# Attention scores two groups ahead of the transposes in a two-block transformer kernel

## The chip, the cores and the metric

The kernel runs on one core of a Trainium2 chip. The metric is the time of one execution on the device in microseconds (us), lower is better. In profile rows PE is TensorE, PEld its weight loads, DVE VectorE, ACT ScalarE, POOL GpSimd and SP SyncE.

## The reference, cut to what matters

Two transformer blocks run one after the other over 512 tokens of width 1024. The change lies in the mixing part of the first block, which is computed for each of its two layers.

```python
def first_block(x, norm_mix, w_in, q_norm, ...):
    for l in range(DEPTH):                       # DEPTH = 2
        h = rmsnorm(x, norm_mix[l])
        proj = jnp.einsum('btd,de->bte', h, w_in[l])
        q, k, v, u, ug, ga, gb = jnp.split(proj, SPLITS, axis=-1)
        ...
        a_out = sliding_window_attention(q, k, v, sinks[l])   # window 128, 16 heads, 2 kv heads
        c_out = conformer_conv(u, ug, conv_w[l], ...)         # 31 taps, layernorm, silu, w_pw
        merged = jax.nn.sigmoid(ga) * a_out + jax.nn.sigmoid(gb) * c_out
        x = x + jnp.einsum('btd,de->bte', merged, w_out[l])
        ...                                      # gated feed-forward
```

In the attention a query block of 128 tokens sees its own and the previous block of keys; the first block of a sequence has no previous one. The softmax has one extra logit for each head, the sink.

## The kernel before, in words

**Layout.** Channels lie on the 128 partitions and tokens on the free axis. Weights stream in as 351 chunks of 128x1024. ScalarE rounds each to `wh` (`round_chunk`), GpSimd subtracts to get the rest `wl` (`rest`), and TensorE multiplies a chunk (`tile`) as 8 x 3 products of 128x512 into one of the eight PSUM banks. Semaphores order the engines; each engine runs its own list of instructions as written, so the code's order is the engine's order.

**Stages of a layer.** Eight chunks for the convolution's input `u`, one for `k`, eight for `q`, one for `v`, sixteen gate chunks, four for the convolution's output (`out(0)` to `out(7)`, two halves of a chunk each, operand `ch` and `cl`), eight for `w_out`, then the feed-forward part.

**The convolution's taps.** Channel tiles 2 and 3 and part of tile 0 are summed on VectorE, one instruction a tap, into banks 6, 7 and 5 (`taps`). The first `SPLIT` taps of tile 0 and all of tile 1 are products on ScalarE (`products`) and additions on GpSimd (`add_tap`). `conv_ready` counts tiles 2, 3 and the joined tile 0.

**Attention groups.** There are 16 groups g of four heads and one block n = g % 4. For each, TensorE computes the scores (`scores`, into banks 0 and 1 or 2 and 3 in turn), VectorE the maxima (`maxima`), ScalarE the exponentials (`exps`), VectorE normalises `prob` (`normalise`), TensorE transposes it into banks 4 and 5, ScalarE copies that out (`turned_out`), TensorE multiplies with `v` in bank 7, and ScalarE copies the result (`pv_out`). A group with n = 0 has one key block, and half the work.

**What is woven in.** Between the transposes of a group and its product with `v` TensorE computes one gate tile in bank 6. VectorE reads it (`gate`, signals `gate_free`), ScalarE takes its tanh and then rounds the next chunk. The layer norm of the convolution (sum, mean, squares, variance, root, product, silu, rounding to `ch`, rest `cl`) is spread over groups 4 to 10, its two sums of TensorE also in bank 6. In the last three groups the output tiles `out(m)` take the gate tiles' place in bank 6: VectorE frees the bank with `gate_conv(m)` (signal `co_out`), and `out(m + 1)` waits for that. Then come `merge`, `merged_hi` and `merged_rest`, which make the operand of `w_out`.

In the lines that follow `LN_EARLY` is 2 and `CO_FROM` 13.

```python
for g in range(16):                       # TensorE, before, without the layer norm
    if g < 15:
        scores(g + 1)
    if g >= CO_FROM:
        out(2 * (g - CO_FROM), 6)
    ...                                   # transposes of group g
    if 1 <= g < CO_FROM:
        tile(c, c % RW, 6, hh, hl)        # gate tile g + 3
    if g >= CO_FROM:
        out(2 * (g - CO_FROM) + 1, 6)
    ...                                   # product of group g with v
```

## Time and profile before

| | us |
|---|---|
| median of three runs | 2336.82 (2336.79 to 2336.86) |
| the profiled execution | 2334.86 |
| its span, first to last instruction | 2332.6 |
| TensorE busy | 2271.0 (97%) |
| VectorE busy | 1137.1 (49%) |
| ScalarE busy | 993.5 (43%) |
| GpSimd busy | 981.8 (42%) |

The span leaves out what lies around the first and last instruction. Matmuls overlap, so a busy TensorE is not one at its peak; what a waiting TensorE loses is read from its idle time. The attention groups of layer 0 lie from 157 to 311 us of the span, those of layer 1 from 869 to 1024 us. A last column in square brackets is the idle time of the engine ahead of a row and what ended it.

### The profile page before, as it was taken

The page shows a single profiled execution, that of the slowest core. Times are in us where ns is not written, and L with a number is a line of the kernel's source. Part 1 is how long each engine was busy: PE and PEld are TensorE (multiplying, and loading weights), DVE is VectorE, ACT ScalarE, POOL GpSimd, SP SyncE. Part 2 cuts the span into 40 slices and gives each one's busy share as a digit, 9 for nine tenths or more (in the row PEclk, how much of TensorE's full clock was granted, in tenths as well). Part 3 has the DMA queues.
Part 4 walks back from the last instruction along what each step waited for, and adds up shares of the span by engine and source line. Part 5 has one row for each costly group of instructions (what it writes and reads, how often), then busy time and mean ns, then how long its engine had stood idle before and what let it go on. Part 6 is the DMA issues. An engine that isn't in the chain of part 4 may idle for free.

```text
span 2332.6 us, 29198 instructions
## 1 busy us (share of the span) xinstructions
PE 2271.0 (97%) x10536; PEld 1791.9 (77%) x10560; DVE 1137.1 (49%) x1475; ACT 993.5 (43%) x1499; POOL 981.8 (42%) x453
## 2 busy tenths in 40 slices
PE   6989999999999999999999999999999999999999
PEld 5866678888888876678888888876777667888887
DVE  5876664222334785666222334647776443433300
ACT  4546643333223545744333213335535663444311
POOL 4962234444443882234444443432442113544442
PEclk9999999999999999999999999999999999999999
DMA  4321123333662221122333472322121002333332
GB/s 151 91 64 56 62 73 91 99 92 97 192 221 73 90 73 54 55 70 88 96 98 98 150 247 90 91 81 64 55 83 53 28 28 72 107 93 97 99 92 88
DMA packets 59842, 216.00 MB, mean 93 GB/s; under 512 B 6640, under 2 KB 6896, under 8 KB 59760
## 3 DMA queue, kind: packets, MB, share of 16 engines
q1 hardware_dynamic: 52272, 187.62, 26.0%
q10 hardware_dynamic: 7488, 27.27, 3.5%
q8 instruction: 54, 0.88, 0.2%
q14 instruction: 28, 0.23, 0.0%
HBM read 212.76 MB, written 2.10 MB: 92 GB/s over the span
## 4 chain that ended last, share of the span: by engine, by line
PE 88%; DVE 7%; ACT 4%; issue 2%; DMA 0%; SPq 0%; DVEq 0%; ACTq 0%
PE bank L1276 26%; PE bank L1278 25%; PE bank L1277 25%; PE bank L1732 1%; PE bank L1410 1%; PE bank L1289 1%; PE bank L1736 1%; PE bank L1470 1%; PE bank L1350 1%; PE bank L1450 1%; PE bank L1720 1%; PE bank L1345 1%; PE bank L1306 1%; ACT prob L479 1%; DVE root L749 1%
## 5 line engine op out<-in xcount | busy, mean ns | idle before, releaser
L307 POOL TENSOR_TENSOR wl<-raw,wh 128x1024 fp32r<-128x1024 f32 x351 | 855.7, 2438 | 1304.3 <-ACT wh L380 1304.1
L1276 PE MATMUL bank<-hh,wh 128*128 128x512 f32 x2024 | 816.3, 403 | 32.9 <-DVE hl L763 19.4
L1277 PE MATMUL bank<-hl,wh 128*128 128x512 f32 x2024 | 792.9, 392 | 0.0
L1278 PE MATMUL bank<-hh,wl 128*128 128x512 f32 x2024 | 792.8, 392 | 0.0
L380 ACT ACTIVATE wh<-raw 128x1024 fp32r<-128x1024 f32 x351 | 369.7, 1053 | 641.8 <-PE bank L1278 610.0
L1276 PEld LDWEIGHTS bank<-hh,wh 128*128 128x128 f32 x2024 | 383.1, 189 | 128.7 <-issue 28.6
L1277 PEld LDWEIGHTS bank<-hl,wh 128*128 128x128 f32 x2024 | 383.2, 189 | 86.3 <-issue 9.8
L1278 PEld LDWEIGHTS bank<-hh,wl 128*128 128x128 f32 x2024 | 382.7, 189 | 81.4
L1276 PE MATMUL bank<-ah,wh 128*128 (+1 forms) x528 | 208.0, 394 | 0.0
L1278 PE MATMUL bank<-ah,wl 128*128 (+1 forms) x528 | 207.0, 392 | 0.0
L1277 PE MATMUL bank<-al,wh 128*128 (+1 forms) x528 | 204.9, 388 | 0.0
L1007 DVE TENSOR_TENSOR tmp<-bank,rstd 128x512 f32<-128x512 f32 x44 | 30.4, 692 | 198.3 <-PE bank L1278 198.3
L327 POOL TENSOR_TENSOR conv<-conv,th 128x512 f32<-128x512 f32 x90 | 118.3, 1315 | 17.4 <-ACT th L428 10.5
L1278 PEld LDWEIGHTS bank<-ah,wl 128*128 128x128 f32 x528 | 99.1, 188 | 23.2
L1277 PEld LDWEIGHTS bank<-al,wh 128*128 128x128 f32 x528 | 99.1, 188 | 22.2
L1276 PEld LDWEIGHTS bank<-ah,wh 128*128 128x128 f32 x528 | 99.3, 188 | 19.7
L796 DVE SCALAR_TENSOR_TENSOR bank<-glu,par,bank 128x512 f32<-128x512 f32 x148 | 111.6, 754 | 4.0
L549 ACT ACTIVATE ah<-tmp 128x512 f32 x44 | 27.8, 632 | 193.8 <-DVE tmp L1010 193.8
L1019 DVE SCALAR_TENSOR_TENSOR ada_acc<-ada_w,cond,ada_acc 128x1024 f32<-128x1024 f32 x42 | 59.3, 1412 | 94.4 <-DMA ada_w<-ada 94.1
L1005 DVE TENSOR_TENSOR tmp<-bank,rstd 128x512 f32<-128x512 f32 x44 | 30.4, 692 | 101.2 <-PE bank L1278 100.7
L479 ACT ACTIVATE prob<-bank,neg_max,q_scale 128x256 f32<-128x256 f32 (+1 forms) x128 | 67.2, 542 | 19.7 <-DVE neg_max L885 19.7
L546 ACT ACTIVATE tmp<-tmp 128x512 f32<-128x512 f32 x44 | 27.8, 632 | 109.5 <-DVE tmp L1005 109.5
(318 smaller groups left out, 2571.9 us busy)
## 6 DMA issues: line engine op xcount, KB each, us to landing
raw<-stream SPq DMA_DIRECT2D x351, 512.0 KB, 3.6
ada_w<-ada ACTq DMA_DIRECT2D x48, 512.0 KB, 4.6
x<-x_t ACTq DMA_DIRECT2D x4, 512.0 KB, 7.8
out_t<-x SPq DMA_DIRECT2D x8, 256.0 KB, 2.1
cst<-consts SPq DMA_DIRECT2D x1, 640.0 KB, 11.1
tmp<-masks SPq DMA_DIRECT2D x1, 320.0 KB, 11.3
par<-params SPq DMA_DIRECT2D x1, 253.0 KB, 4.6
cst<-consts SPq DMA_DIRECT2D x1, 224.0 KB, 8.0
```

Of the source, the lines that this page charges most:

```text
L307: nc.gpsimd.tensor_tensor(wl[:, slot, :], raw[:, raw_slot, :], wh[:, slot, :].bitcast(F32), ALU.subtract).then_inc(lo_ready, 1)
L327: nc.gpsimd.tensor_tensor(conv[:, tile_, :], conv[:, tile_, :], th[:, 0, 4 + (p - 1 - tile_) % 4, :], ALU.add).then_inc(tap_added, 1)
L380: af(wh[:, slot, :], raw[:, raw_slot, :], ACT.Copy).then_inc(hi_ready, 1)
L479: af(prob[:, g % 2, i, lo:], bank[:, b + kv, (i % 2) * 2 * P + lo:(i % 2 + 1) * 2 * P], ACT.Exp, bias=neg_max[:, g % 2, i:i + 1], scale=q_ ...
L546: af(tmp[:, 2 + p, :], tmp[:, 2 + p, :], ACT.Silu).then_inc(ffn_silu, 1)
L796: link(stt(acc, glu[:, t, j:j + T], w, acc, ALU.mult, ALU.add))
L1005: tt(tmp[:, 2 + p, :], bank[:, b, :], rstd[:, :], ALU.mult).then_inc(lin_free, 1)
L1007: tt(tmp[:, 4 + p, :], bank[:, b + 1, :] if b < 3 else bank[:, 0, :], rstd[:, :], ALU.mult).then_inc(lin_free, 1)
L1019: stt(acc, w, c_k, acc, ALU.mult, ALU.add).then_inc(ada_used, 1)
L1276: mm(dst, wh[:, slot, w], xh, start=start, stop=False)
L1277: mm(dst, wh[:, slot, w], xl, start=False, stop=False)
L1278: return mm(dst, wl[:, slot, w], xh, start=False, stop=stop)
```

## The change

Scores, maxima, exponentials and normalising run two groups ahead of the transposes instead of one, and TensorE issues the next scores behind the transposes of a group instead of ahead of them. Two gate tiles instead of three are computed ahead of the first scores; tiles 2 and 3 follow the first two score groups, in banks 6 and 4. The layer norm is spread over groups 3 to 12. Tile 0 of the convolution gives 20 instead of 16 taps to ScalarE and GpSimd. In the last three groups VectorE normalises ahead of `gate_conv`. The code that is left out of the diff repeats these edits.

```diff
@@ -222,8 +222,8 @@
...
-        EARLY_GATES = 3
-        CO_FROM = 16 - EARLY_GATES
+        EARLY_GATES, AHEAD = 2, 2
+        CO_FROM = 13
...
@@ -236,15 +236,16 @@
...
-        TAPS_U, TAPS_Q = [2, 3, 4, 4, 4, 4], [4, 4, 3, 3, 5, 5, 5, 5]
-        SPLIT, LN_EARLY = 16, 2
+        TAPS_U, TAPS_Q = [2, 3, 4, 2, 4, 5], [5, 4, 3, 4, 5, 5, 5, 5]
+        SPLIT = 20
...
-        PRODUCTS_AT = {2: 3, C_K: 2, C_Q: 4, C_V: 2, C_GATE: 2, C_GATE + 1: 2, C_GATE + 2: 1}
+        PRODUCTS_AT = {2: 3, C_K: 2, C_Q: 4, C_V: 4, C_GATE: 2, C_GATE + 1: 3, C_GATE + 2: 2}
...
-        ADDS_AT = {2: 1, C_K: 2, C_V: 2, C_GATE: 2, C_GATE + 1: 2, C_GATE + 2: 2}
+        ADDS_AT = {2: 1, C_K: 2, C_V: 4, C_GATE: 2, C_GATE + 1: 4, C_GATE + 2: 2}
...
+        LN_SUM, LN_MEAN, LN_SQUARES, LN_VAR, LN_ROOT, LN_NORM, LN_HI, LN_REST = 3, 5, 6, 8, 9, 10, 11, 12
...
@@ -490,6 +491,10 @@
...
                 exps(0)
+                exps(1)
+                gate(2)
+                products(C_GATE + 2)
+                gate(3)
                 for g in range(16):
...
-                    if g < 15:
-                        exps(g + 1)
-                    if g == 7 - LN_EARLY:
...
-                    if g == 9 - LN_EARLY:
...
-                    if g == 11 - LN_EARLY:
...
-                    if g == 12 - LN_EARLY:
...
-                    else:
-                        gate(g + EARLY_GATES)
+                    elif g:
+                        gate(g + 3)
...
@@ -868,8 +873,6 @@
...
                 gate(1, M_V % 4)
-                taps(5)
-                gate(2, M_SWAP[7] % 4)
                 taps(len(own) - tapped[0])
                 join_split()
...
                 maxima(0)
+                maxima(1)
+                gate(2, 6)
                 normalise(0)
+                normalise(1)
+                gate(3, 4)
                 for g in range(16):
...
-                    if g < 15:
-                        maxima(g + 1)
-                    if g == 6 - LN_EARLY:
...
-                    if g == 7 - LN_EARLY:
...
+                    if g == LN_SQUARES:
...
-                    if g == 10 - LN_EARLY:
+                    if g == LN_ROOT:
                         invert(tmp[:, 5, :], root[:, :])
-                    if g == 11 - LN_EARLY:
...
+                    if g + AHEAD < 16:
+                        normalise(g + AHEAD)
                     if g < CO_FROM:
-                        normalise(g + 1)
-                        if g == 12 - LN_EARLY:
+                        if g:
+                            gate(g + 3, 6)
+                        if g == LN_REST:
                             for t in range(CT):
                                 out_rest(t)
-                        gate(g + EARLY_GATES, 6)
...
-                        if g < 15:
-                            normalise(g + 1)
                         merge(m + 1)
...
@@ -1387,7 +1394,6 @@
                 last.then_inc(vt_turned, 1)
                 tile(c0 + C_GATE + 1, (c0 + C_GATE + 1) % RW, M_V % 4, hh, hl)
                 pe.wait_ge(lin_free, m0 + M_SWAP[7] + 1)
-                tile(c0 + C_GATE + 2, (c0 + C_GATE + 2) % RW, M_SWAP[7] % 4, hh, hl)
...
                 scores(0)
-                pe.wait_ge(conv_ready, (CT - 1) * l + 2)
-                tile(c0 + C_GATE + EARLY_GATES, (c0 + C_GATE + EARLY_GATES) % RW, 6, hh, hl)
+                scores(1)
+                pe.wait_ge(conv_ready, (CT - 1) * l + 1)
+                tile(c0 + C_GATE + 2, (c0 + C_GATE + 2) % RW, 6, hh, hl)
                 pe.wait_ge(root_ready, ROOTS * l + 3)
+                tile(c0 + C_GATE + 3, (c0 + C_GATE + 3) % RW, 4, hh, hl)
                 for g in range(16):
                     n, j = group(g)
-                    if g == 7 - LN_EARLY:
...
-                        pe.wait_ge(gate_free, 16 * l + g + EARLY_GATES)
...
-                    if g < 15:
-                        scores(g + 1)
                     if g >= CO_FROM:
                         out(2 * (g - CO_FROM), 6)
                     pe.wait_ge(probs_ready, 16 * l + g + 1)
-                    if g:
+                    if g == 0:
+                        pe.wait_ge(conv_ready, (CT - 1) * (l + 1))
+                    else:
                         pe.wait_ge(turned_out, 16 * l + g)
+                    if g == 1:
+                        pe.wait_ge(gate_free, 16 * l + 4)
                     for w in range(1 if n == 0 else 0, 2):
...
                     last.then_inc(turned, 1)
-                    if g == 7 - LN_EARLY:
+                    if g + AHEAD < 16:
+                        scores(g + AHEAD)
+                    if g == LN_MEAN:
                         pe.wait_ge(mean_out, l + 1)
-                    if g == 9 - LN_EARLY:
+                    if g == LN_VAR:
...
                     if 1 <= g < CO_FROM:
-                        pe.wait_ge(gate_free, 16 * l + g + EARLY_GATES)
-                        c = c0 + C_GATE + g + EARLY_GATES
+                        pe.wait_ge(gate_free, 16 * l + g + 3)
+                        c = c0 + C_GATE + g + 3
                         tile(c, c % RW, 6, hh, hl)
...
-                    if g == 0:
-                        pe.wait_ge(conv_ready, (CT - 1) * (l + 1))
```

**TensorE at the start of the groups**, from the first scores to the first product with `v`. `win_mask` rows open a score group, `k,q` rows are scores, `hh,wh` opens a gate tile, `cst,prob` rows are transposes and `prob_t,v` the product. Before:

```order
L1405 MATMUL bank<-win_mask,ident_bf 128x512 [waits lin_free,gate_free,k_ready,consts_ready]
...
L1410 MATMUL bank<-k,q 128x128 x4
L1276 MATMUL bank<-hh,wh 128x512 [waits lo_ready,conv_ready]
...
L1405 MATMUL bank<-win_mask,ident_bf 128x512 [waits gate_free,root_ready]
...
L1450 MATMUL bank<-cst,prob 128x128 [waits probs_ready]
...
L1470 MATMUL bank<-prob_t,v 64x256 [waits turned_out,conv_ready]
```

And now:

```order
L1411 MATMUL bank<-win_mask,ident_bf 128x512 [waits lin_free,k_ready,gate_free,consts_ready]
...
L1411 MATMUL bank<-win_mask,ident_bf 128x512 [waits gate_free]
...
L1416 MATMUL bank<-k,q 128x256 x4
L1283 MATMUL bank<-hh,wh 128x512 [waits lo_ready,conv_ready]
...
L1283 MATMUL bank<-hh,wh 128x512 [waits lo_ready,root_ready]
...
L1460 MATMUL bank<-cst,prob 128x128 [waits conv_ready,probs_ready]
...
L1411 MATMUL bank<-win_mask,ident_bf 128x512 [waits exp_ready]
...
L1480 MATMUL bank<-prob_t,v 64x256 [waits turned_out]
```

The second score group moved ahead of the gate tiles, a second gate tile stands behind the first, and the third score group stands between the transposes and the product. Whether the tile waits for the first or the second tile of `conv` is a number in the wait that the rows do not print.

**TensorE at group 13**, from the product of group 12 to the start of `out(1)` (`ch,wh` rows open or go on with an output tile). Before:

```order
L1470 MATMUL bank<-prob_t,v 64x256 [waits pv_out,turned_out]
...
L1405 MATMUL bank<-win_mask,ident_bf 128x512 [waits exp_ready]
...
L1410 MATMUL bank<-k,q 128x256 x4
L1276 MATMUL bank<-ch,wh 128x512 [waits cl_ready,gate_free,lo_ready]
...
L1450 MATMUL bank<-cst,prob 128x128 [waits turned_out,probs_ready]
L1450 MATMUL bank<-cst,prob 128x128 x7
L1276 MATMUL bank<-ch,wh 128x512 [waits co_out,lo_ready]
```

And now:

```order
L1480 MATMUL bank<-prob_t,v 64x256 [waits pv_out,turned_out]
...
L1283 MATMUL bank<-ch,wh 128x512 [waits cl_ready,gate_free,lo_ready]
...
L1460 MATMUL bank<-cst,prob 128x128 [waits turned_out,probs_ready]
L1460 MATMUL bank<-cst,prob 128x128 x7
L1411 MATMUL bank<-win_mask,ident_bf 128x512 [waits exp_ready]
...
L1416 MATMUL bank<-k,q 128x256 x4
L1283 MATMUL bank<-ch,wh 128x512 [waits co_out,lo_ready]
```

The score group, 14 before and 15 now, moved from ahead of `out(0)` to directly ahead of `out(1)`.

**VectorE at group 13**, from the maxima to `gate_conv(1)` (`row_max` to `sink_arg` are the maxima, `den` to `prob` the normalising, `th<-th,bank` is `gate_conv`, `tmp<-th,q` is `merge`). Before:

```order
L882 TENSOR_REDUCE row_max<-bank 128x4 [waits scores_ready]
...
L887 TENSOR_TENSOR sink_arg<-par,neg_max 128x4 [waits max_ready]
L912 SCALAR_TENSOR_TENSOR th<-th,bank 128x512 [waits gate_tanh,co_ready]
L920 TENSOR_TENSOR tmp<-th,q 128x512 [waits gated,co_out]
L912 SCALAR_TENSOR_TENSOR th<-th,bank 128x512 [waits gate_tanh,used]
L893 TENSOR_TENSOR den<-den,sink_exp 128x4 [waits exp_ready]
L894 RECIPROCAL rden<-den 128x4 [waits dve_linked]
L896 TENSOR_TENSOR prob<-prob,rden 128x1024 [waits dve_linked]
```

And now:

```order
L885 TENSOR_REDUCE row_max<-bank 128x4 [waits scores_ready]
...
L890 TENSOR_TENSOR sink_arg<-par,neg_max 128x4 [waits max_ready]
L896 TENSOR_TENSOR den<-den,sink_exp 128x4 [waits exp_ready]
L897 RECIPROCAL rden<-den 128x4 [waits dve_linked]
L899 TENSOR_TENSOR prob<-prob,rden 128x1024 [waits dve_linked]
L915 SCALAR_TENSOR_TENSOR th<-th,bank 128x512 [waits gate_tanh,co_ready]
L923 TENSOR_TENSOR tmp<-th,q 128x512 [waits gated,co_out]
L915 SCALAR_TENSOR_TENSOR th<-th,bank 128x512 [waits gate_tanh,used]
```

The normalising moved from behind both `gate_conv` to ahead of them.

## Rows read from the trace of the kernel before

**Rows 1.** The page: its first line and busy times (share of span, instructions).

```profile
span 2332.6 us, 29198 instructions
...
PE 2271.0 (97%) x10536; PEld 1791.9 (77%) x10560; DVE 1137.1 (49%) x1475; ACT 993.5 (43%) x1499; POOL 981.8 (42%) x453
```

**Rows 2.** Waits of TensorE: for what; us in total, times, longest.

```profile
PE bank L1450 <- DVE prob L896: 5.8, 6, 2.2
PE bank L1276 <- DVE conv L798: 5.6, 2, 2.8
...
PE bank L1276 <- DVE tmp L862: 3.8, 2, 1.9
PE bank L1276 <- DVE ml L924: 3.6, 2, 1.8
...
PE bank L1436 <- DVE tmp L862: 2.8, 2, 1.4
```

**Rows 3.** Timeline of TensorE, layer 0: start, duration, line, operation.

```profile
160.65 0.50 PE L1276 MATMUL bank<-hh,wh 128*128 128x512 f32 x1 [2.78 <-DVE conv L798]
...
166.22 0.60 PE L1405 MATMUL bank<-win_mask,ident_bf 128*128 128x512 bf16 x2
166.76 1.13 PE L1410 MATMUL bank<-k,q 64*128 64x256 f32 x8
167.82 0.66 PE L1450 MATMUL bank<-cst,prob 128*128 128x128 f32 x4
169.25 0.65 PE L1470 MATMUL bank<-prob_t,v 128*64 128x256 f32 x4 [0.78 <-ACT prob_t L500]
...
173.70 1.09 PE L1450 MATMUL bank<-cst,prob 128*128 128x128 f32 x8 [2.19 <-DVE prob L896]
174.55 0.48 PE L1276 MATMUL bank<-hh,wh 128*128 128x512 f32 x1
...
180.18 1.08 PE L1470 MATMUL bank<-prob_t,v 128*64 128x256 f32 x8
...
289.71 0.47 PE L1276 MATMUL bank<-ch,wh 128*128 128x512 f32 x1 [0.26 <-DVE th L912]
```

**Rows 4.** Timeline of VectorE, group 1 of layer 0; last, the page's GpSimd additions.

```profile
167.94 1.22 DVE L882 TENSOR_REDUCE row_max<-bank 128x4 f32<-128x1024 f32 x1 [1.74 <-PE bank L1410]
...
173.56 0.68 DVE L862 TENSOR_TENSOR tmp<-bank,rstd 128x512 f32<-128x512 f32 x1
...
L327 POOL TENSOR_TENSOR conv<-conv,th 128x512 f32<-128x512 f32 x90 | 118.3, 1315 | 17.4 <-ACT th L428 10.5
```

**Rows 5.** Timeline of GpSimd and of VectorE, layer 0, two places and a reference.

```profile
183.34 2.39 POOL L307 TENSOR_TENSOR wl<-raw,wh 128x1024 fp32r<-128x1024 f32 x1 [5.01 <-ACT wh L380]
...
184.17 1.57 DVE L884 TENSOR_TENSOR row_max<-row_max,q_minus 128x4 f32<-128x4 f32 x1
...
250.13 4.70 DVE L956 TENSOR_TENSOR conv<-conv,tmp 128x512 f32<-128x512 f32 x4
...
265.84 2.49 DVE L904 TENSOR_TENSOR cl<-conv,ch 128x512 fp32r<-128x512 f32 x4
```

**Rows 6.** Timeline of ScalarE: the root of the variance; a gate's tanh; GpSimd behind.

```profile
234.03 1.28 ACT L509 ACT_TABLE_LOAD   x1
235.33 0.63 ACT L509 ACTIVATE root<-tmp 128x512 f32<-128x512 f32 x1
...
284.48 0.63 ACT L463 ACTIVATE th<-tmp 128x512 f32<-128x512 f32 x1 [2.30 <-DVE tmp L862]
...
286.13 2.41 POOL L307 TENSOR_TENSOR wl<-raw,wh 128x1024 fp32r<-128x1024 f32 x1 [6.60 <-ACT wh L380]
```

**Rows 7.** Timeline of TensorE; then windows: length, busy by engine, granted clock, DMA.

```profile
1966.55 0.77 PE L1276 MATMUL bank<-hh,wh 128*128 128x512 f32 x1 [3.73 <-issue]
...
872.00:876.00 4.00, 3.60 (x9) 2.89 (x10) 3.90 (x6) 1.15 (x5) 3.86 (x3) 0.57 0.33 85
1966.00:1972.00 6.00, 5.45 (x14) 4.37 (x15) 6.00 (x10) 3.04 (x5) 0.00 (x0) 0.54 0.28 87
```

More of the change, by code:

```diff
@@ L500, in _ @@
                     af(prob_t[:, 1, :, :], bank[:, 5, :].rearrange("p (a b) -> p a b", a=4), ACT.Copy).then_inc(turned_out, 1)
-                    if g < 15:
-                        exps(g + 1)
-                    if g == 7 - LN_EARLY:
+                    if g + AHEAD < 16:
+                        exps(g + AHEAD)
+                    if g == LN_MEAN:
                         for t in range(CT):
@@ L513, in _ @@
                             af(conv[:, t, :], conv[:, t, :], ACT.Silu, bias=par_l(l, "ln_b", t), scale=par_l(l, "ln_g", t)).then_inc(silu_ready, 1)
-                    if g == 12 - LN_EARLY:
+                    if g == LN_HI:
                         for t in range(CT):
@@ L926, in _ @@
                 maxima(0)
+                maxima(1)
+                gate(2, 6)
                 normalise(0)
+                normalise(1)
+                gate(3, 4)
                 for g in range(16):
-                    if g == 7 - LN_EARLY:
+                    if g == LN_MEAN:
                         dve.wait_ge(mean_ready, l + 1)
                         ts(tmp[:, 5, :], bank[:, 6, :], -1.0 / (CT * P), None, ALU.mult).then_inc(mean_out, 1)
-                    if g == 9 - LN_EARLY:
+                    if g == LN_VAR:
                         dve.wait_ge(ln_summed, l + 1)
                         ts(tmp[:, 5, :], bank[:, 6, :], 1.0 / (CT * P), EPS, ALU.mult, ALU.add).then_inc(var_out, 1)
-                    if g < 15:
-                        maxima(g + 1)
-                    if g == 6 - LN_EARLY:
+                    if g + AHEAD < 16:
+                        maxima(g + AHEAD)
+                    if g == LN_SUM:
                         dve.wait_ge(tap_added, N_ADDS * (l + 1))
@@ L942, in _ @@
                         tt(tmp[:, 5, :], tmp[:, 4, :], tmp[:, 5, :], ALU.add).then_inc(conv_summed, 1)
-                    if g == 7 - LN_EARLY:
+                    if g == LN_MEAN:
                         dve.wait_ge(mean_out, l + 1)
@@ L951, in _ @@
                         tt(tmp[:, 0, :], tmp[:, 0, :], tmp[:, 4, :], ALU.add).then_inc(sq_used, CT)
-                    if g == 10 - LN_EARLY:
+                    if g == LN_ROOT:
                         invert(tmp[:, 5, :], root[:, :])
-                    if g == 11 - LN_EARLY:
+                    if g == LN_NORM:
                         for t in range(CT):
@@ L1427, in _ @@
                 scores(0)
-                pe.wait_ge(conv_ready, (CT - 1) * l + 2)
-                tile(c0 + C_GATE + EARLY_GATES, (c0 + C_GATE + EARLY_GATES) % RW, 6, hh, hl)
+                scores(1)
+                pe.wait_ge(conv_ready, (CT - 1) * l + 1)
+                tile(c0 + C_GATE + 2, (c0 + C_GATE + 2) % RW, 6, hh, hl)
                 pe.wait_ge(root_ready, ROOTS * l + 3)
+                tile(c0 + C_GATE + 3, (c0 + C_GATE + 3) % RW, 4, hh, hl)
                 for g in range(16):
                     n, j = group(g)
-                    if g == 7 - LN_EARLY:
+                    if g == LN_MEAN:
                         pe.wait_ge(conv_summed, l + 1)
-                        pe.wait_ge(gate_free, 16 * l + g + EARLY_GATES)
+                        pe.wait_ge(gate_free, 16 * l + g + 3)
                         mm(bank[:, 6, :], ones, tmp[:, 5, :], start=True, stop=True).then_inc(mean_ready, 1)
-                    if g == 9 - LN_EARLY:
+                    if g == LN_VAR:
                         pe.wait_ge(sq_used, s0 + SQ_LN + CT)
-                        pe.wait_ge(gate_free, 16 * l + g + EARLY_GATES)
+                        pe.wait_ge(gate_free, 16 * l + g + 3)
                         mm(bank[:, 6, :], ones, tmp[:, LN_TMP[0], :], start=True, stop=True).then_inc(ln_summed, 1)
-                    if g < 15:
-                        scores(g + 1)
                     if g >= CO_FROM:
@@ L1451, in _ @@
                     last.then_inc(turned, 1)
-                    if g == 7 - LN_EARLY:
+                    if g + AHEAD < 16:
+                        scores(g + AHEAD)
+                    if g == LN_MEAN:
                         pe.wait_ge(mean_out, l + 1)
-                    if g == 9 - LN_EARLY:
+                    if g == LN_VAR:
                         pe.wait_ge(var_out, l + 1)
                     if 1 <= g < CO_FROM:
-                        pe.wait_ge(gate_free, 16 * l + g + EARLY_GATES)
-                        c = c0 + C_GATE + g + EARLY_GATES
+                        pe.wait_ge(gate_free, 16 * l + g + 3)
+                        c = c0 + C_GATE + g + 3
                         tile(c, c % RW, 6, hh, hl)
```

3 lines of the change are left out of this document (2 added, 1 removed).

## The prediction

> **What bounds the kernel now.** I read the page first: TensorE is busy for 97% of the span [rows 1], so a change pays only where it removes or adds time in which TensorE stands still, or in which its clock is low. The list of waits of TensorE is therefore the second view. Its lines that lie in the attention stages, which this change rewrites, are few [rows 2]: 5.6 us for `conv` of the convolution, 5.8 us for the normalised `prob`, 3.8 and 2.8 us for a gate tile that VectorE has not read (L862), 3.6 us for `ml` at the end. Half of each sum belongs to each layer. The timeline shows where they stand in layer 0 [rows 3]: 2.78 us before the first gate tile in bank 6, 0.78 us before the first product with `v`, 2.19 us before the transposes of group 1, 0.26 us before `out(1)`. The other `prob` waits (0.7 us), the wait ahead of the mean (1.4 us) and one ahead of gate tile 14 (1.9 us) come later. Without `ml` a layer waits 2.78 + 0.78 + 2.9 + 1.4 + 1.9 + 0.26 = 10.0 us. This is all that the change can win, 20.0 us in two layers, plus a piece of clock in layer 1.
>
> Third, the chain of one group on VectorE and ScalarE [rows 4]: scores end at 167.89 (166.76 + 1.13 in [rows 3]), VectorE starts the row maxima at 167.94, and behind the exponentials of ScalarE and the normalising it is free for its next instruction at 173.56. That is 5.7 us from the end of the scores, whatever stands behind it.
>
> **What it removes.** Gate tile 2 goes to bank 6 behind two score groups and waits only for the first `conv_ready`, so the 2.78 us go. The transposes of a group now stand a full gate tile behind its scores: 5.63 us for a tile (174.55 to 180.18), 0.85 us for eight transposes (173.70 to 174.55) and 1.60 us for a full score group (166.22 to 167.82), all [rows 3], give over 14 us for a chain of 5.7 us, so the 2.9 us for `prob` go. `out_rest` moves behind `gate`, so the 1.9 us go. TensorE's instructions are as many as before. The four taps go off VectorE as four more additions on GpSimd and products on ScalarE. They cost nothing: they run under the query and gate tiles, and [rows 2] has no wait of TensorE for a tap or an addition there; without that cover four additions are 5.3 us a layer (1315 ns each, the last of [rows 4]).
>
> **What it adds, per layer.**
> (a) The first product with `v` needs `turned_out` of group 0, which ScalarE now does behind gate 3 and a rounded chunk. Tile 3 ends, VectorE reads it (0.7 us), ScalarE needs 1.5 us and the copy 0.6 us, while TensorE has only 2.0 us of transposes and scores. That waits 1.0 us; behind late exponentials 2.2. I take 1.5.
> (b) The mean (LN_MEAN still at group 5) waits for gate 7 as before: with the sum moved away, 0.7 (0.4 to 1.4).
> (c) Gate 12 or 14 late at tiles 13 and 15: 0.2 (0 to 0.9).
> (d) `out(0)` used to stand behind the scores of the next group. Now it comes at once after tile 15 and a short product: 6.2 us after the scores, where gate 15 is read at 6.4 at best and the first `cl` is there at 7.1: 1.0 us. Two things push it. GpSimd's subtraction holds off VectorE's two-operand work: a `row_max` product of 128x4 took 1.57 us and ended as the subtraction did (185.74 and 185.73), and four `conv` products took 4.70 us where four like them took 2.49 [rows 5]. And at the variance ScalarE loads two tables (1.28 us each) and takes a root of 0.63 us before its gate [rows 6]; the subtraction starts 1.65 us after that gate's tanh (284.48 to 286.13), so a late tanh puts it on the next group's maxima, up to 2.3 us a group. Carried by hand from group 8 to group 12, gate 15 ends 1.5 to 2.3 us late. I take 2.6 (1.0 to 3.3).
> (e) The last `out_rest` begins within 0.1 us of that subtraction. If it loses, `out(0)` waits 2.0 us more; I take 1.0 (0 to 2.0).
> (f) The largest: `out(1)` needs `gate_conv(0)`, which frees bank 6. Before, that was VectorE's first work behind the maxima of group 14. Now VectorE at group 13 does maxima(15) and normalise(15) first, and scores(15) are issued only after `out(0)` and the transposes, directly ahead of `out(1)`. TensorE has nothing in between. It stands for the whole chain, 5.7 us [rows 4], and the product of 0.7 us: 6.4 us. GpSimd's subtraction can add up to 1.4 of the 1.57 in [rows 5], so 6.3 to 7.8.
> Behind it everything finds its order again; the 1.8 us for `ml` stay.
> Sum: 1.5 + 0.7 + 0.2 + 2.6 + 1.0 + 6.4 = 12.4 us (8.7 to 17.6) against 10.0: +2.4 a layer (-1.3 to +7.6), +4.8 in all (-2.6 to +15.2).
>
> **The clock.** The granted clock was 0.57 from 872 to 876, in layer 1, behind the 2.78 us wait, which lost (1 - 0.57) x 4 = 1.7 us; layer 0, behind the same wait, ran its tile in 5.6 us at full clock. After the longer wait of 3.73 us, it was 0.54 from 1966 to 1972, 2.8 us lost [rows 7]. (f) is longer than both, in both layers, so I expect a fall to the lower level, 1.2 GHz, each time, at 2.1 us; the old one goes: 4.2 - 1.7 = +2.5 (-1.7 to +3.9).
> Total +7.3 us: span 2332.6 to 2339.9, that execution's time 2334.9 to 2342.2. The median of the runs is 2.0 us above it, so the forecast is 2344.1 us.
>
> The Trainium skill bears on two prices. Its page "SBUF — State Buffer", section "Who interferes with whom", says that a VectorE instruction with two SBUF inputs contends with a GpSimd instruction that reads SBUF; by that rule, [rows 5] agree, and (d) and (e) stay; were they nothing, the sum would be 2.6 us a layer less. Its page "ScalarE: Activation LUTs", section "What ACT_TABLE_LOAD costs", gives some 2.66 us for a switch with the drain; the trace has the root starting 1.30 us after the load does [rows 6], and the trace's figure is used. By the page's the tanh at the variance would come 2.7 us later, and (d) would be near its upper end, 0.7 us a layer more.
>
> **The rivals.**
> 1. The wait at `out(1)` is real, but the gate groups run to time: (a) 1.0, (b) 0.4, (d) 1.0, (e) 0 and (f) 6.4, with a clock fall in each layer of 1.7. That is 8.8 us a layer, -2.4 in two, +1.7 for the clock: -0.7, 2336 us. For it: before, most groups met their gate at the tile's end. Against: the subtraction met the maxima in about half of the groups. It decides if gate 15 is read within 0.5 us of tile 15's end. Between it and my case lie all values up to 2341.5. Chance 0.25.
> 2. Faster, on one mechanism: the clock does not fall behind (f), as it did not in layer 0 behind 2.78 us. From rival 1's waits this gives -2.4 - 1.7 = -4.1, and with (b) hidden -4.9, 2332 us. It decides where the granted clock stays 1.00 behind `out(1)`'s wait. Against it: of the three waits in [rows 3, 7] only one of 2.78 us left the clock up, and the longest did not. Chance 0.07.
> 3. Much slower: the clock falls a second time, behind (d) or (a), and GpSimd's subtraction lands in (f): all upper ends, 15.2 + 3.9 = +19 us, 2356 us. Chance 0.05.
> 4. That the waits at the start do not go: excluded by the order, the tile there needs no late `conv`.
> My forecast, 2341.5 to 2353 us: 0.63.
>
> **How the numbers follow.** What this kernel can tell from no change is about 0.2%, 4.7 us. Slower by more, above 2341.5: 0.63 + 0.05 = 0.68. Within: 0.25. Faster: 0.07. The range 2335 to 2353 us takes in my case and rival 1 down to a little under its own time, and leaves out the faster one, the third and the lowest part of rival 1, less than 0.2 in all. The likeliest case's own range is 2341.5 to 2350.
>
> **What the profile after would show.** A wait for `th` (the line of `gate_conv`) of 6.4 us before a `ch` tile, twice; it shows (f). None for `conv` before the gate tile, none for `prob`. A wait for `cl` or the gate ahead of `out(0)` of 2 to 4 us (d, e). A granted clock near 0.5 behind `out(1)`'s start in both layers. I am wrong if the wait at `th` is under 5 us (VectorE got there earlier than I read), if the waits at (d) and (e) are near 1 us, or if the low clock is missing.

## The result, and the profile after

The changed kernel takes 2348.58 us (median of 6 runs, 2344.29 to 2350.51) against 2336.84 us (6 runs, 2335.55 to 2342.49): ratio 1.004, 95% interval 1.003 to 1.005. It is slower by 0.4%, 9.4 us by the ratio (7 to 12). The profiled execution took 2348.56 us, 1.9 us more than its span. First its page, which answers to [rows 1], then its waits of TensorE, which answer to [rows 2]: for what, us in total, times, longest.

```profile
span 2346.7 us, 29246 instructions
...
PE 2285.6 (97%) x10560; PEld 1801.9 (77%) x10560; DVE 1137.9 (48%) x1467; ACT 998.5 (43%) x1507; POOL 994.6 (42%) x461
```

```profile
PE bank L1283 <- DVE th L915: 13.0, 2, 6.5
PE bank L1283 <- DVE cl L907: 6.1, 2, 3.1
...
PE bank L1283 <- DVE ml L927: 2.5, 2, 1.2
...
PE bank L1480 <- ACT prob_t L505: 1.9, 2, 0.9
...
PE bank L1444 <- DVE tmp L867: 1.0, 2, 0.5
```

The waits for `conv` in the attention stage and for `prob` are gone. In their place stand 6.5 us a layer ahead of `out(1)` (`th`, line 915, is `gate_conv`) and 3.1 us ahead of `out(0)` (`cl`). TensorE's timeline of layer 0 shows the places: start, duration, line, operation, and in brackets the idle time and what ended it.

```profile
172.49 0.65 PE L1480 MATMUL bank<-prob_t,v 128*64 128x256 f32 x4 [0.94 <-ACT prob_t L505]
...
184.81 0.50 PE L1283 MATMUL bank<-hh,wh 128*128 128x512 f32 x1 [0.38 <-DVE tmp L867]
...
209.65 1.10 PE L1444 MATMUL bank<-tmp,cst 128*128 128x512 f32 x2 [0.52 <-DVE tmp L867]
...
281.99 0.65 PE L1480 MATMUL bank<-prob_t,v 128*64 128x256 f32 x4
285.70 0.47 PE L1283 MATMUL bank<-ch,wh 128*128 128x512 f32 x1 [3.06 <-DVE cl L907]
286.01 0.46 PE L1284 MATMUL bank<-cl,wh 128*128 128x512 f32 x1
286.26 0.63 PE L1285 MATMUL bank<-ch,wl 128*128 128x512 f32 x1
...
291.51 1.13 PE L1416 MATMUL bank<-k,q 64*128 64x256 f32 x8
299.14 0.77 PE L1283 MATMUL bank<-ch,wh 128*128 128x512 f32 x1 [6.50 <-DVE th L915]
299.71 0.63 PE L1284 MATMUL bank<-cl,wh 128*128 128x512 f32 x1
...
303.43 0.39 PE L1284 MATMUL bank<-cl,wh 128*128 128x512 f32 x1
```

Two things are to be read here. The scores of group 15 start at 291.51 and `out(1)`, the next product, at 299.14: TensorE has nothing between them. And the same 128x512 product lasts 0.63 us behind both waits, and 0.39 us once the clock is back. Windows show it (start:end, length, busy time of PE, PEld, DVE, ACT, POOL with instructions, granted clock, DMA share, GB/s).

```profile
286.00:290.00 4.00, 4.00 (x12) 3.13 (x11) 1.36 (x3) 0.84 (x2) 2.95 (x1) 0.57 0.00 0
296.00:304.00 8.00, 4.86 (x14) 3.61 (x14) 2.85 (x5) 1.37 (x6) 0.00 (x0) 0.57 0.00 0
1002.00:1006.00 4.00, 2.80 (x7) 2.26 (x8) 2.86 (x5) 1.85 (x3) 1.86 (x1) 0.63 0.00 0
1013.00:1020.00 7.00, 3.44 (x8) 2.79 (x9) 2.86 (x5) 1.78 (x6) 0.00 (x0) 0.52 0.00 0
```

So the clock falls to its lower level, 1.2 GHz, behind `out(0)` and again around `out(1)`, in both layers; each of these windows takes in some time at full clock, so its mean lies above 0.50. VectorE's timeline of the last groups, with one row of GpSimd's, says why the two waits are as long as they are.

```profile
277.65 2.40 POOL L308 TENSOR_TENSOR wl<-raw,wh 128x1024 fp32r<-128x1024 f32 x1 [6.60 <-ACT wh L381]
```

```profile
277.70 2.37 DVE L887 TENSOR_TENSOR row_max<-row_max,q_minus 128x4 f32<-128x4 f32 x1
...
283.13 1.22 DVE L899 TENSOR_TENSOR prob<-prob,rden 128x1024 f32<-128x1024 f32 x1
284.27 0.68 DVE L867 TENSOR_TENSOR tmp<-bank,rstd 128x512 f32<-128x512 f32 x1
284.87 2.49 DVE L907 TENSOR_TENSOR cl<-conv,ch 128x512 fp32r<-128x512 f32 x4
...
292.69 1.22 DVE L885 TENSOR_REDUCE row_max<-bank 128x4 f32<-128x1024 f32 x1 [5.33 <-PE bank L1416]
293.95 0.16 DVE L887 TENSOR_TENSOR row_max<-row_max,q_minus 128x4 f32<-128x4 f32 x1
...
296.77 0.16 DVE L896 TENSOR_TENSOR den<-den,sink_exp 128x4 f32<-128x4 f32 x1 [2.26 <-ACT sink_exp L483]
...
297.18 1.23 DVE L899 TENSOR_TENSOR prob<-prob,rden 128x1024 f32<-128x1024 f32 x1
298.32 0.68 DVE L915 SCALAR_TENSOR_TENSOR th<-th,bank 128x512 f32<-128x512 f32 x1
```

A product of 128x4 that takes 0.16 us elsewhere (293.95) took 2.37 us here, until the subtraction on GpSimd was over at 280.05: group 14 lost 2.2 us, and gate 15 is read at 284.27, 1.6 us behind the end of the short product. For `out(1)` VectorE first stood idle for 5.33 us, since `gate_conv(0)` stands behind maxima(15) in its program and the scores of group 15 come late; then came maxima, exponentials and normalising. Each of the expected steps is there.

### The profile page after: what moved, and what is told of

It reads as the page before. It is cut to its first block, busy times and chain, and to the rows that moved or that the text cites. A ratio compares the mean times of both kernels' runs of the same rounds, so it can differ in the third digit from the quotient of the medians.

```text
span 2346.7 us, 29246 instructions
## 1 busy us (share of the span) xinstructions
PE 2285.6 (97%) x10560; PEld 1801.9 (77%) x10560; DVE 1137.9 (48%) x1467; ACT 998.5 (43%) x1507; POOL 994.6 (42%) x461
## 4 chain that ended last, share of the span: by engine, by line
PE 89%; DVE 5%; ACT 3%; issue 2%; DMA 0%; SPq 0%; DVEq 0%; ACTq 0%
PE bank L1283 26%; PE bank L1285 26%; PE bank L1284 26%; PE bank L1742 1%; PE bank L1416 1%; PE bank L1460 1%; ACT prob L480 1%; PE bank L1480 1%; PE bank L1296 1%; PE bank L1746 1%; PE bank L1357 1%; PE bank L1730 1%; PE bank L1352 1%; DVE root L754 1%; PE bank L1313 1%
## 5 line engine op out<-in xcount | busy, mean ns | idle before, releaser
L328 POOL TENSOR_TENSOR conv<-conv,th 128x512 f32<-128x512 f32 x98 | 128.7, 1313 | 18.5 <-ACT th L429 10.5
L801 DVE SCALAR_TENSOR_TENSOR bank<-glu,par,bank 128x512 f32<-128x512 f32 x140 | 105.5, 754 | 3.8
```

The costliest lines, as they stand in the source:

```text
L328: nc.gpsimd.tensor_tensor(conv[:, tile_, :], conv[:, tile_, :], th[:, 0, 4 + (p - 1 - tile_) % 4, :], ALU.add).then_inc(tap_added, 1)
L801: link(stt(acc, glu[:, t, j:j + T], w, acc, ALU.mult, ALU.add))
```

## The experiments

Each time stands beside runs of the kernel before on the same chip: medians of 2336.86 us for experiments 1 to 4, 2336.67 us for 5 to 7 and 2339.51 us for 9. The changed kernel itself was not timed again beside them, so a difference to it goes by medians of separate sets of runs. In the diffs, `-` is the changed kernel unless something else is said.

**1. The gate first.** In groups 13 to 15 VectorE does `gate_conv(m)` first, ahead of the maxima and of the normalising of the group two ahead.

```diff
                 for g in range(16):
+                    if g >= CO_FROM:
+                        gate_conv(2 * (g - CO_FROM), 6)
...
-                    if g + AHEAD < 16:
+                    if g + AHEAD < 16 and g < CO_FROM:
                         normalise(g + AHEAD)
...
-                        gate_conv(m, 6)
...
                         gate_conv(m + 1, 6)
+                        if g + AHEAD < 16:
+                            normalise(g + AHEAD)
```

> The changed kernel with one part of VectorE's order restored: at groups 13 to 15 gate_conv(m) stands first in the group, and normalise behind gate_conv(m+1). My theory: the 6.5 us in which TensorE waits for gate_conv(0) ahead of out(1) in each layer are VectorE's order alone, so they fall under 0.5 us, and with them the clock fall behind that wait (about 2.1 us a layer). The wait ahead of out(0) stays at 3.1 us. Time: 2 x 6.5 + 2 x 2.1 = 17 us under the changed kernel, about 2331 us, ratio to before 0.997. Rival (the work only moves, and VectorE is too full in the last groups): a wait of 3 us or more appears at out(2), at out(3) or at the transposes of group 15, and the time stays over 2340 us.

Measured: 2328.65 us (6 runs, 2326.15 to 2333.48), ratio 0.9957 (0.9943 to 0.997). The wait ahead of `out(1)` is gone; 0.58 us a layer stands ahead of `out(4)` instead:

```profile
PE bank L1286 <- DVE cl L907: 6.2, 2, 3.1
...
PE bank L1286 <- DVE th L915: 1.2, 2, 0.6
```

Against the changed kernel that is 19.9 us by the medians, where the waits are 11.8 us shorter (13.0 to 1.2). The other 8 us come mostly with the clock (the attention stages take 175.2 and 173.6 us; table under 8): no window behind `out(1)` is below 1.00 in either layer, and behind `out(0)` it fell only in layer 0. The order on VectorE is the cause of the wait. The edit puts `gate_conv(0)` ahead of both the maxima and the normalising, so it does not tell how much each adds; in the rows of the changed kernel 4.4 us lie between the end of the maxima's reduction (293.91) and `th` (298.32).

**2. The scores first.** TensorE does scores(15) ahead of `out(0)`, not behind it.

```diff
                     if g >= CO_FROM:
+                        if g + AHEAD < 16:
+                            scores(g + AHEAD)
                         out(2 * (g - CO_FROM), 6)
...
-                    if g + AHEAD < 16:
+                    if g + AHEAD < 16 and g < CO_FROM:
                         scores(g + AHEAD)
```

> The changed kernel with scores(15) ahead of out(0), VectorE's order as in the change. Two reasons for the wait at out(0) stand against each other: if it is that nothing stands between tile 15 and out(0), 1.6 us of scores take their share and the 3.1 us become about 1.5; if gate 15 itself moves with what TensorE issues, it stays near 3. The exponentials of group 15 need the transposes of group 13, so the chain behind out(1) begins at the transposes instead of at the scores: wait of 4.7 us instead of 6.5. Together 3.4 us a layer, 6.8 us under the changed kernel: 2341 us, ratio 1.002. If the waits were one fixed chain from gate 15 on, both would keep their sum of 9.6 us and the time stay at 2348.

Measured: 2339.59 us (12 runs, 2335.02 to 2341.74), ratio 0.9998 (0.9989 to 1.0007). The scores cover half of the wait ahead of `out(0)` (1.5 us a layer are left), but `out(1)` still waits for 5.8 us, more than was worked out. ScalarE's timeline shows the piece that was missed: its copies of group 13's transposes stand ahead of the exponentials of group 15 in its program, and could start only behind `out(0)`.

```profile
289.02 0.60 ACT L504 ACTIVATE prob_t<-bank 128x512 f32<-128x512 f32 x1 [2.77 <-PE bank L1462]
289.51 0.59 ACT L505 ACTIVATE prob_t<-bank 128x512 f32<-128x512 f32 x1
289.99 0.57 ACT L480 ACTIVATE prob<-bank,neg_max,q_scale 128x256 f32<-128x256 f32 x1
```

Earlier scores thus give little while ScalarE's order stays. That the time is 9 us lower, with waits 4.6 us shorter, is mostly the clock again: one fall a layer in place of two.

**3. The clock alone.** 26 products that nobody reads fill the hole ahead of `out(1)`; everything else is unchanged.

```diff
+                    if g == CO_FROM:
+                        pe.wait_ge(exp_ready, 16 * l + 15)
+                        for i in range(FILL):
+                            mm(bank[:, i % 2, :], hh[:, 0, 0:P], hh[:, 1, :], start=True, stop=True)
                     if g >= CO_FROM:
                         out(2 * (g - CO_FROM) + 1, 6)
```

> The changed kernel with 26 products of 128x512 that nobody reads ahead of out(1) in each layer, in the banks 0 and 1, which are free there: 5.9 us of work within the wait of 6.5. Theory that the low clock comes from TensorE standing still: the granted clock stays at 1.00 behind that wait, the wait for gate_conv(0) is under 1 us, and the time is 2 x 2.1 = 4 us lower than the changed kernel's (about 2344). Rival, that the clock falls there for another reason (the time since the last fall, or the small products of scores and transposes): the clock falls all the same, now during the extra products, and the time is the same or up to 4 us higher.

Measured: 2341.0 us (12 runs, 2337.88 to 2344.14), ratio 1.0007 (0.9997 to 1.0016): 7.6 us less than the changed kernel by the medians, with work added and none taken away. That is nearly twice the 4 us that were expected. The trace shows only a part of it: in the profiled execution, the slowest of the twelve, the attention stages took 181.0 and 182.1 us, 3.1 us less than the changed kernel's means (table under 8). TensorE's timeline and two windows:

```profile
292.07 6.19 PE L1476 MATMUL bank<-hh 128*128 128x512 f32 x26
298.64 0.47 PE L1284 MATMUL bank<-ch,wh 128*128 128x512 f32 x1 [0.39 <-DVE th L916]
```

```profile
281.00:290.00 9.00, 5.92 (x23) 4.17 (x22) 4.84 (x9) 3.13 (x9) 2.95 (x1) 0.81 0.15 55
290.00:306.00 16.00, 15.56 (x78) 11.55 (x78) 6.27 (x12) 5.96 (x15) 1.20 (x1) 1.00 0.12 34
```

Behind the filled hole the clock stays at 1.00; behind the unfilled one ahead of `out(0)` it still falls.

**4. Experiments 1 and 2 together, and the rest a group earlier** (`LN_REST` 11 in place of 12, the diff of both edits is above).

```diff
-        LN_SUM, LN_MEAN, LN_SQUARES, LN_VAR, LN_ROOT, LN_NORM, LN_HI, LN_REST = 3, 5, 6, 8, 9, 10, 11, 12
+        LN_SUM, LN_MEAN, LN_SQUARES, LN_VAR, LN_ROOT, LN_NORM, LN_HI, LN_REST = 3, 5, 6, 8, 9, 10, 11, 11
```

> The changed kernel with three repairs: gate_conv first in groups 13 to 15 on VectorE, scores(15) ahead of out(0) on TensorE, and the rest for cl at group 11 instead of 12. Theory: the wait at out(1) goes (6.5 us), that at out(0) falls from 3.1 to about 1, and the clock falls behind both go (1.7 and 2.1 us): 2 x (6.5 + 2.1 + 3.8) = 25 us under the changed kernel, about 2323 us, ratio 0.994: faster than the kernel before. Rival, that looking two groups ahead costs as much elsewhere as it wins: not under 2333 us.

Measured: 2323.44 us (6 runs, 2320.84 to 2327.08), ratio 0.9935 (0.9922 to 0.9948), faster than both kernels. `out(0)` starts 1.41 us late, without a releaser that the profile names, `out(4)` waits for 0.58 us, and in both attention stages the clock is at 1.00 throughout. So the rest of the change is worth having once the two holes are closed; which part of it brings the gain was not separated, except that the taps alone (5) bring none.

**5. The taps alone.** The kernel before with only the tap tables of the change.

```diff
-        TAPS_U, TAPS_Q = [2, 3, 4, 4, 4, 4], [4, 4, 3, 3, 5, 5, 5, 5]
-        SPLIT, LN_EARLY = 16, 2
+        TAPS_U, TAPS_Q = [2, 3, 4, 2, 4, 5], [5, 4, 3, 4, 5, 5, 5, 5]
+        SPLIT, LN_EARLY = 20, 2
```

> The kernel before with one part of the change: 20 instead of 16 taps of tile 0 on ScalarE and GpSimd, with the change's tables. The wait of 2.78 us for conv ahead of the gate tile in bank 6 is VectorE's last taps; four fewer at 0.78 us are 3.1 us, so it goes in both layers without any look-ahead, and with it the clock fall of 1.7 us in layer 1. The waits for prob (2.19) stay. 2 x 2.78 + 1.7 = 7.3 us under the kernel before: 2329.6 us, ratio 0.997. Rival (the taps only cost nothing, the look-ahead won the 2.8 us): the wait stays over 1.5 us, since GpSimd's additions or ScalarE's products are late in their turn, and the time is that of the kernel before within 2 us.

Measured: 2335.86 us (11 runs, 2333.47 to 2338.32), ratio 0.9994 (0.9985 to 1.0004): no difference. The wait for `conv` went (5.6 us), but the waits for `prob` grew, from 5.8 to 7.1 us:

```profile
PE bank L1450 <- DVE prob L896: 7.1, 8, 1.9
```

One step beyond the wait explains it. GpSimd now adds from 156.17 to 161.74 and subtracts and adds on behind that, and VectorE's small sum and the first normalising are held at 162.19 and 164.34 (1.90 us and 1.51 us, where the same shapes take 0.16 and 0.69 us):

```profile
162.19 1.90 DVE L893 TENSOR_TENSOR den<-den,sink_exp 128x4 f32<-128x4 f32 x1 [1.87 <-ACT sink_exp L482]
...
164.34 1.51 DVE L896 TENSOR_TENSOR prob<-prob,rden 128x512 f32<-128x512 f32 x1
```

That accounts for 1.3 us. The rest went, in this execution, to falls of the clock: 0.83 from 170 to 180 and from 880 to 890, behind waits for `prob`, and 0.91 from 260 to 280, behind the old wait ahead of gate tile 14; 5.2 us lost where [rows 7] had 1.7. Experiment 8 shows that such falls differ between executions of one kernel, so this trace alone does not tie them to the edit. What was worked out counted only the wait.

**6. No table loads at the variance.** Tanh stands in place of the root, so the values are not those of a layer norm; the time is what counts.

```diff
-                        af(root[:, :], tmp[:, 5, :], ACT.Sqrt).then_inc(root_ready, 1)
+                        af(root[:, :], tmp[:, 5, :], ACT.Tanh).then_inc(root_ready, 1)
```

> The changed kernel with a tanh in place of the layer norm's root, which leaves the root out of the computation and with it two loads of tables on ScalarE at group 8. My step (d) says that the late gate 15 was carried from there: then the wait ahead of out(0) falls from 3.1 to about 1 us and the clock stays up behind it, 2 x (2.1 + 1.7) = 7.6 us under the changed kernel (2341). Rival, that it comes from the silu's loads at groups 10 and 11 or is made anew in each group: the wait stays at 3.1 us, time 2346 to 2350.

Measured: 2340.98 us (10 runs, 2338.49 to 2344.12), ratio 1.0016 (1.0007 to 1.0026). The wait ahead of `out(0)` is 1.76 us in place of 3.06, where about 1 was expected; `out(1)` waits for 6.50 us, as in the changed kernel. VectorE's timeline shows that the subtraction, which starts at 275.47 here, still holds it, but on another operation:

```profile
275.04 0.16 DVE L887 TENSOR_TENSOR row_max<-row_max,q_minus 128x4 f32<-128x4 f32 x1
...
275.70 3.32 DVE L903 SCALAR_TENSOR_TENSOR q<-th,q 128x512 f32<-128x512 f32 x2
```

The two operations of the last row (`gate_attention`) take 1.29 us in the changed kernel. The subtraction starts 1.68 us behind the start of the maxima here and 1.21 us in the changed kernel: it misses the small product because it is later, not earlier.

**7. A short subtraction.** From gate tile 3 on, GpSimd subtracts 8 of 1024 columns, so that the lower halves of those weights are left out.

```diff
-                    rest(c + RW, (c + RW) % RW, (c + RW) % RR)
+                    rest(c + RW, (c + RW) % RW, (c + RW) % RR, 8 if i >= C_GATE + 3 else D)
```

> The changed kernel with GpSimd's subtraction cut to 8 of 1024 columns for the chunks that are rounded from gate 3 of the attention groups on, which leaves out most of their rest. Theory: the products of 128x4 on VectorE that take up to 2.4 us wait for GpSimd's hold on the memory; they go back to 0.2 us, gate 15 is read at the tile's end, the wait ahead of out(0) falls to about 1 us and the wait for gate_conv(0) stays 6.5. Time 2341 us. Rival, that ScalarE's late exponentials set gate 15, and VectorE's products wait for something else: the wait stays over 2.5 us.

Measured: 2338.42 us (10 runs, 2335.53 to 2340.41), ratio 1.0002 (0.9993 to 1.0012). The wait ahead of `out(0)` is 0.89 us; the product at 277.70 above, which took 2.37 us, takes 0.16 us. Experiments 6 and 7 overlap: they take 1.3 and 2.2 us off a wait of 3.06. The hold is thus shown to cause most of this wait. That the loads matter is shown too, but by which steps between group 8 and group 13 is not, and the step that was expected, a late tanh that puts the subtraction on the maxima, is not what the rows of experiment 6 show.

**8. The two kernels executed again.** Two more executions of each, without any edit, and between them the changed kernel with both holes filled.

> The kernel before once more, for the part of the time that the clock takes outside the attention stages. Its own trace lost 3.5 us of clock in the first 40 us, that of the changed kernel 8.5, over the same instructions. If that is chance of the single execution, this trace shows another value than 3.5 or the list of times spreads by a few us (2335 to 2342); if it belongs to the kernel, it is 3.5 again.

> The changed kernel unaltered, looked at a second time. Theory (waits are fixed by the program, the falls of the clock partly by the execution): the waits of TensorE are the same row for row within 0.1 us (0.94, 0.39, 0.52, 3.06, 6.50, 1.2 us a layer), and the clock lost in the attention stages, 10.2 us in the first execution, lies between 6 and 12 us. Rival (the falls belong to the waits alone): 10.2 us again within 0.5, and the same 22 us outside these stages.

> The kernel before unaltered, a third look, for one question: the first product with v_t of layer 0 began at 145.24 and 145.48 us in two executions of this kernel and at 149.72 and 149.22 us in two of the changed one, though TensorE's instructions ahead of it are the same in both; in other variants it began at 145.2, 147.0 or 149.3. Theory (chance of the execution): one of these three values, not bound to the kernel. Rival (bound to the program): 145.2 to 145.5 again. The waits of TensorE are the same row for row by both.

> The changed kernel unaltered, a third look. Theory (chance of the execution): the first product with v_t begins at 145.2, 147.0 or 149.3 us. Rival (bound to the program): 149.2 to 149.8 again. Its attention stages take 182.5 to 184.4 us each, from that product to the wait for ml, with two falls of the clock in each.

Measured: the kernel before took 2342.8 and 2336.53 us, the changed one 2350.7 and 2344.82 us. The waits of the attention stages repeat row for row within 0.1 us. The clock does not. One stretch of the attention stage of layer 0, in the first and the second execution of the kernel before:

```profile
160.00:180.00 20.00, 16.23 (x83) 11.93 (x84) 11.25 (x24) 10.05 (x33) 6.54 (x4) 1.00 0.13 34
```

```profile
160.00:180.00 20.00, 16.15 (x65) 11.64 (x66) 10.91 (x22) 7.70 (x26) 5.43 (x4) 0.76 0.08 26
```

The same waits for `conv` and `prob` left the clock at 1.00 once, and cost (1 - 0.76) x 20 = 4.8 us by the window the next time (4.4 us by the length of the stage, below). To set it apart, the span is cut at two rows of TensorE's timeline that both kernels have in each layer: the first product with `v_t`, and the product that waits for `ml`. In the first execution of each:

```profile
145.24 0.60 PE L1386 MATMUL bank<-cst,v_t 128*128 128x128 f32 x4
...
323.59 0.50 PE L1276 MATMUL bank<-mh,wh 128*128 128x512 f32 x1 [1.81 <-DVE ml L924]
```

```profile
149.72 0.60 PE L1393 MATMUL bank<-cst,v_t 128*128 128x128 f32 x4
...
332.60 0.50 PE L1283 MATMUL bank<-mh,wh 128*128 128x512 f32 x1 [1.22 <-DVE ml L927]
```

| us | before, three executions | changed, three | changed, both holes filled |
|---|---|---|---|
| start to `v_t`, layer 0 | 145.24, 145.48, 146.77 | 149.72, 149.22, 145.23 | 147.21 |
| attention stage, layer 0 | 178.35, 182.78, 178.45 | 182.88, 182.52, 183.32 | 179.48 |
| between them | 533.43, 533.80, 533.54 | 534.62, 535.08, 534.21 | 534.17 |
| attention stage, layer 1 | 179.93, 182.92, 179.89 | 182.52, 184.34, 182.94 | 179.47 |
| rest of the span | 1295.6, 1295.6, 1295.6 | 1297.0, 1297.6, 1297.2 | 1295.1 |
| clock lost, start to `v_t` | 3.5, 3.4, 5.1 | 8.5, 8.6, 3.4 | 5.1 |
| clock lost, between the stages | 3.4, 3.4, 3.4 | 5.1, 5.2, 5.1 | 5.1 |

The start differs by up to 4.5 us between executions of the changed kernel, and the third of each kernel crosses over, so the expectation that tied it to the program fell. The last two rows, sums of (1 - granted clock) x 10 us over windows of 10 us, say what it is: in all fourteen traces a start with 3.4 to 3.5 us lost takes 145.2 to 145.5 us, one with 5.1 or 5.2 takes 146.8 to 147.2, and one with 8.5 or 8.6 takes 149.2 to 149.7. The stretch between the attention stages behaves alike: seven traces with 3.4 us lost between 720 and 750 take 533.4 to 533.9 us there, and seven with 5.1 or 5.2 take 534.2 to 535.1. Both groups hold variants of both kernels' programs: experiments 1, 3, 4 and 7 are in the first, experiment 5, made from the kernel before, in the second.

The same traces show how often the clock was low just behind a hole of the last groups, by the windows of 3 us from its end: behind 5.8 to 6.5 us in 12 holes of 12, behind 3.05 to 3.09 us in 9 of 10 (the exception is layer 1 of experiment 1), behind 1.73 and 1.76 us in 1 of 2, and behind 0.38 to 1.5 us in none of 14.

**9. Both holes filled.** Experiment 3, with 12 more unread products ahead of `out(0)`.

```diff
+                    if g == CO_FROM:
+                        pe.wait_ge(exp_ready, 16 * l + 14)
+                        for i in range(FILL_0):
+                            mm(bank[:, 2 + i % 2, :], hh[:, 0, 0:P], hh[:, 1, :], start=True, stop=True)
```

> The changed kernel with unread 128x512 products in both holes of each layer: 12 of them (2.9 us at 0.238 us each) ahead of out(0), 26 (6.2 us) ahead of out(1). They change no other instruction and fill time in which TensorE stood still. Theory (what the changed kernel loses beyond its waits is the clock that falls behind both waits): with one filler the kernel took 2341.0 us and still lost 1.7 us of clock behind out(0) in layer 0 and 3.4 us in layer 1. With both, the granted clock stays 1.00 there, and the time is 3.4 to 5.1 us lower, 2336 to 2338 us, the time of the kernel before (ratio 1.000). Rival (the surplus that was left lies elsewhere, at the start of the program): 2341 us again, ratio 1.0018. Second rival: the fall moves behind another wait; then a window of low clock stands elsewhere in the attention stages.

Measured: 2338.18 us (11 runs, 2337.05 to 2342.0), ratio 1.0002 (0.9993 to 1.0011): the time of the kernel before. What the second filler adds to experiment 3 (1.0007, 0.9997 to 1.0016) is within the noise of the times; the traces show it. Windows around the two holes, of the changed kernel and of this one:

```profile
275.00:310.00 35.00, 25.45 (x113) 18.54 (x112) 18.52 (x29) 14.34 (x35) 7.72 (x3) 0.85 0.09 30
990.00:1025.00 35.00, 25.44 (x116) 17.96 (x115) 17.82 (x29) 15.79 (x41) 6.01 (x3) 0.85 0.14 44
```

```profile
275.00:310.00 35.00, 34.42 (x166) 25.47 (x166) 19.27 (x31) 14.63 (x36) 8.56 (x4) 1.00 0.15 45
990.00:1025.00 35.00, 34.44 (x168) 25.45 (x168) 19.24 (x32) 14.21 (x34) 8.74 (x4) 1.00 0.15 46
```

`out(0)` and `out(1)` start as late after the scores as ever; only the clock is different. Without its falls behind the two holes the changed kernel is not measurably slower than the kernel before, which has falls of its own in these stages.

## Why the prediction was right, and where its sizes were not

The forecast was 2344.1 us, slower; the median is 2348.58. Step by step, per layer:

- **What goes.** All of it went as worked out: `conv`, `prob`, the wait ahead of tile 14 and the 0.26 us ahead of `out(1)`.
- **(f), 6.4 us (6.3 to 7.8).** 6.50 us in both layers, by the chain named; experiment 1 shows that VectorE's order is the cause. The subtraction did not fall on these maxima (0.16 us at 293.95).
- **(d), 2.6 us, and (e), 1.0 us.** Together 3.06 where 3.6 was taken: (e) did not occur (the `cl` operations ran unhindered, 2.49 us for four, from 284.87), and (d) is 3.06, near its upper end of 3.3. Both things that were named matter: without the loads 1.76 us are left, without the subtraction's hold 0.89, near the 1.0 that was worked out as the least. The route between them, a late tanh, is not shown (experiments 6 and 7). Where the `cl` operations met the subtraction, at 286.64, it was the subtraction that took longer, 2.95 us in place of 2.40.
- **(a), 1.5 us:** 0.94. The exponentials were not late; the lower price of 1.0 was right. **(b), 0.7 us:** 0.52. **(c), 0.2 us:** 0.38, at gate tile 5 (184.81), not at 13 or 15. **`ml`, 1.8 us as before:** 1.2.
- **The sum of the waits** was the first mis-sized term: 11.4 us, and with `ml` 12.6 against 11.8 before, +0.8 a layer where +2.4 was forecast (1.6 us in all for 4.8). Rival 1, which put the gate groups on time, had the waits of (a) and (e) right and (d) wrong.
- **The clock** was the second. The prediction counted one fall a layer, behind (f), at 2.1 us, and against it one old fall of 1.7 us in the whole kernel. There were two falls a layer, behind (d) too. Taking the kernel with both holes filled as the attention stage at full clock (179.5 us), the changed kernel loses 183.1 - 179.5 = 3.6 us a layer (means of six stages). The kernel before, whose stages without a fall take 178.4 us, loses 180.4 - 178.4 = 2.0 us a layer on average, not 0.85. Two of its three profiles lose about 1.5 us in all and one 8.9; the prediction had one of the two quick ones, and 33 of 71 times of this kernel, over the four sets of runs, lie above 2339 us, behind a gap from 2338.1 to 2339.3. On average over three executions the clock is thus net +3.2 us in all for the forecast's +2.5; against the one execution that the prediction read it is +5.0. Rival 3 had the second fall right, and its place; its upper ends for the waits were not reached.
- **The whole.** In three executions of each, the span is 10.3 us longer on average (2346.1 against 2335.8). The attention stages are 5.4 us of it: 3.2 of clock as above, and 2.2 of waits (1.6 by the rows of the waits). The start is 2.2 us and the stretch between the stages 1.1 us; both go with the clock as the table under 8 shows, and neither is bound to the changed program, though with three executions each a small difference of the means is not excluded. The last 1.6 us stand in the rest of the span. With the holes filled that takes 1295.1 us, less than in either kernel; through what, no run here shows.
- **Luck.** The direction and its cause came as forecast; that the size came near did not follow from the sum. In the first execution of each kernel the attention stages differ by 7.1 us, where 7.3 were forecast, but as 2.2 of waits and 5.0 of clock for 4.8 and 2.5: two misses of opposite sign. On average these stages give 5.4 us, and the other 4.9 us of the span stand where the prediction put nothing.

What is shown: the order on VectorE causes the wait at `out(1)`; GpSimd's hold causes most of the one at `out(0)`, and the table loads play a part in it; idle time ahead of those two tiles brings the clock down, since it stayed at 1.00 behind all six holes that were filled. What stays open is why the clock falls in one execution and not in another, how the loads act, and the last 1.6 us.

## What to carry to other kernels

When a producer is moved one step ahead on one engine, walk the same step through the in-order programs of the other engines, down to the last groups: here a stage that was moved ahead everywhere left VectorE's gate behind a chain whose input TensorE issued last, and moving that gate to the head of its group turned a loss of 0.4% into a gain of 0.4%. Price a hole on TensorE of 3.06 or 6.5 us as that length plus a fall of the clock of some 1.8 us (3.6 us for the two of a layer), and count the old holes too, with the share of executions in which the clock falls behind them. A single profile samples the clock's falls; before 5 us are explained, look at two or three executions and cut the span at rows that both kernels have.

## What the runs showed of the hardware

- The waits are a property of the program, the falls of the clock of the execution too: identical waits lost nothing or 4.8 us in the window from 160 to 180.
- TensorE's clock can be held with products that nobody reads: 26 of 128x512 in a hole of 6.5 us, and 12 in one of 3.1 us, kept the granted clock at 1.00 and took 10.4 us off the time (2348.58 to 2338.18, by the medians; 8.9 us by the ratios to the kernel before, 1.004 and 1.0002).
- A GpSimd subtraction of 2.40 us held even the smallest VectorE operation with two inputs: 128x4 took 2.17 us (at 268.90) and 2.37 us (at 277.70) in place of 0.16, and with 8 of 1024 columns subtracted 0.16 again.
- ScalarE's table loads can cost TensorE time far behind them: without two of them (1.28 us each) at group 8, a wait of TensorE five groups later was 1.3 us shorter.
